# Hybrid diffusion step on one core: ScalarE copies the first pass of the second feed-forward product, and one first product takes high parts first

## What is computed

```python
def sq_relu_mlp(h, w1, w2):
    return jnp.square(jax.nn.relu(h @ w1)) @ w2
...
    for layer in range(DEPTH):
        ...
        hp = modulate(rmsnorm(xp, norm_ffn_pre[layer]), mod_p[3], mod_p[4])
        hs = modulate(rmsnorm(xs, norm_ffn_pre[layer]), mod_s[3], mod_s[4])
        xp = xp + mod_p[5] * rmsnorm(sq_relu_mlp(hp, w_ffn_in[layer], w_ffn_out[layer]), norm_ffn_post[layer])
        xs = xs + mod_s[5] * rmsnorm(sq_relu_mlp(hs, w_ffn_in[layer], w_ffn_out[layer]), norm_ffn_post[layer])
```

## Time and profile before

| what | value |
|---|---|
| median of 3 runs | 1427.66 us (1427.63 to 1428.13) |
| the profiled execution's own time | 1429.37 us |
| its span in the trace | 1427.3 us |
| TensorE matmuls busy | 1373.6 us, 96% |
| VectorE busy | 885.5 us, 62% |
| GpSimd busy | 715.1 us, 50% |
| ScalarE busy | 706.2 us, 49% |
| mean granted TensorE clock | 0.988 |

### The profile page before, as it was taken

The page is one execution under the profiler, slowest core; times in us unless marked ns, Lnnn a source line. Parts: engine busy times, 40 slices in busy tenths (PEclk is TensorE's granted clock), DMA queues, the critical chain, the costliest instruction groups (busy, mean ns, idle before and its releaser), DMA issues.

```text
span 1427.3 us, 20872 instructions
## 1 busy us (share of the span) xinstructions
PE 1373.6 (96%) x7682; PEld 1162.0 (81%) x7682; DVE 885.5 (62%) x1543; ACT 706.2 (49%) x1431; POOL 715.1 (50%) x547
## 2 busy tenths in 40 slices
PE   5999999989999999999999989999899999999998
PEld 3876787868888888989767867788789899899896
DVE  4477864866655565565663578627855655656646
ACT  4375824744434444443552367637544534444443
POOL 1430413775445556555352567635855565555550
PEclk8999999999999999999999999999999999999999
DMA  9534272533454412212455200034323222231213
GB/s 350 161 95 142 69 257 68 192 118 119 136 209 157 148 59 90 89 62 87 153 185 185 89 2 1 1 118 172 108 90 104 74 91 87 72 106 59 89 60 148
DMA packets 98059, 164.32 MB, mean 115 GB/s; under 512 B 11100, under 2 KB 49704, under 8 KB 97960
## 3 DMA queue, kind: packets, MB, share of 16 engines
q1 hardware_dynamic: 86320, 157.23, 32.4%
q10 hardware_dynamic: 11640, 5.76, 1.6%
HBM read 154.82 MB, written 8.16 MB: 114 GB/s over the span
## 4 chain that ended last, share of the span: by engine, by line
PE 45%; DVE 2%; POOL 2%; issue 1%; ACT 0%; DVEq 0%; POOLq 0%; ACTq 0%
PE PS L2025 13%; PE PS L2026 13%; PE PS L2027 13%; PE PS L2367 2%; PE PS L2356 1%; PE PS L2335 1%; PE PS L2075 1%; PE PS L2336 1%; PE PS L2319 0%; PE PS L2312 0%; POOL WLU L1592 0%; POOL GG L1538 0%; PE PS L2115 0%; POOL HL L1561 0%; DVE HF L1786 0%
## 5 line engine op out<-in xcount | busy, mean ns | idle before, releaser
L1592 POOL TENSOR_TENSOR WLU<-RAW,WHU 128x512 fp32r<-128x512 f32 x340 | 457.5, 1371 | 376.3 <-ACT WHU L1227 376.2
L1227 ACT CAST WHU<-RAW 128x512 fp32r<-128x512 f32 x340 | 197.3, 618 | 236.9 <-PE PS L2027 121.7
L2025 PE MATMUL PS<-WHU,MXR 128*128 128x512 f32 x640 | 254.6, 398 | 11.9 <-issue 9.8
L2026 PE MATMUL PS<-WLU,MXR 128*128 128x512 f32 x640 | 252.0, 394 | 0.0
L2027 PE MATMUL PS<-WHU,MXR 128*128 128x512 f32 x640 | 251.6, 393 | 0.0
L1934 DVE TENSOR_TENSOR ACC<-ACC,PS 128x512 f32<-128x512 f32 x260 | 177.6, 684 | 94.8 <-PE PS L2027 93.7
L1587 POOL TENSOR_TENSOR WL<-RAW,WH 128x512 fp32r<-128x512 f32 x84 | 117.5, 1432 | 212.9 <-ACT WH L1218 195.4
L2025 PE MATMUL PS<-HH,WHU 128*128 128x320 f32 (+2 forms) x576 | 178.8, 310 | 3.9 <-POOL HL L1561 3.9
L2027 PE MATMUL PS<-HH,WLU 128*128 128x320 f32 (+2 forms) x576 | 178.6, 310 | 0.0
L2026 PE MATMUL PS<-HL,WHU 128*128 128x320 f32 (+2 forms) x576 | 178.5, 310 | 0.0
L2025 PEld LDWEIGHTS PS<-WHU,MXR 128*128 128x128 f32 x640 | 121.1, 189 | 47.2 <-issue 17.9
(11 more groups left out here) (274 smaller groups left out, 2637.3 us busy)
## 6 DMA issues: line engine op xcount, KB each, us to landing
RAW<-in_w_ffn_in SPq DMA_DIRECT2D x32, 1024.0 KB, 5.5
RAW<-in_w_ffn_out SPq DMA_DIRECT2D x32, 1024.0 KB, 5.0
RAW<-in_w_mod SPq DMA_DIRECT2D x18, 1024.0 KB, 5.8
GG<-in_w_mod SPq DMA_DIRECT2D x13, 1024.0 KB, 7.4
MX<-in_w_mod SPq DMA_DIRECT2D x11, 1024.0 KB, 5.2
RAW<-in_w_in_even SPq DMA_DIRECT2D x7, 1024.0 KB, 5.3
RAW<-in_w_qkv SPq DMA_DIRECT2D x6, 1024.0 KB, 7.5
xd<-X SPq DMA_DIRECT2D x10, 512.0 KB, 8.0
```

What stands on the lines that cost most here:

```text
L1227: nc.scalar.copy(unit_view(WHU, u), unit_raw(u["ld"], u["of"])).then_inc(u_hi, 1)
L1592: nc.gpsimd.tensor_tensor(unit_view(WLU, u), unit_raw(u["ld"], u["of"]), unit_view(WHU, u).bitcast(f32), ALU.subtract)\
L2025: MM(out, wh, xh, start=first, stop=False, skip_group_check=reopens)
L2026: MM(out, wh, xl, start=False, stop=False, skip_group_check=reopens)
```

## The change

ScalarE takes over the ten copies of the first pass. The planner holds unit S3 of pair 2 back to event 16 (group 8 of the first pass; before, event 13 was the least). The direct product of p = 0, f = 0, part 1 waits for the high parts of its tokens alone, does its 16 matmuls on them, and then the 8 with the low parts of the tokens.

```diff
                     at = max(at, cycle + 9 if o[0] > 2 else NS + 5)
                 if o == (2, "S2"):
                     at = max(at, NS + 2)
+                if o == (2, "S3"):
+                    at = max(at, NS + 8)
...
+                elif k == "g" and not s["p"]:
+                    b = s["b"]
+                    act.wait_ge(t_add, 12 * s["layer"] + 12)
+                    upto(act, b_ready, b)
+                    nc.scalar.copy(ACC[:, s["t"], 512 * s["nh"]:512 * s["nh"] + 512], PS[:, 4 + b % 2, :]).then_inc(b_free[b % 2], 1)
...
-                elif k == "g":
+                elif k == "g" and s["p"]:
                     b, acc = s["b"], ACC[:, s["t"], 512 * s["nh"]:512 * s["nh"] + 512]
                     upto(dve, b_ready, b)
-                    if not s["p"]:
-                        dve.wait_ge(t_add, 12 * s["layer"] + 12)
-                    if s["p"]:
-                        V_.tensor_tensor(acc, acc, PS[:, 4 + b % 2, :], ALU.add).then_inc(b_free[b % 2], 1)
-                    else:
-                        V_.tensor_copy(acc, PS[:, 4 + b % 2, :]).then_inc(b_free[b % 2], 1)
+                    V_.tensor_tensor(acc, acc, PS[:, 4 + b % 2, :], ALU.add).then_inc(b_free[b % 2], 1)
...
-                    if p == 0 and f == 0:
+                    out = direct_bank(s)
+                    if (p, f, part) == (0, 0, 1):
+                        cols = DIRECT[1]
+                        for i in (0, 1):
+                            u = s["units"][i]
+                            pe.wait_ge(u_lo, u["number"] + 1)
+                            pe.wait_ge(f_hi[i], TT * layer + 5)
+                            for kt in range(4):
+                                for w in (WHU, WLU):
+                                    MM(out, unit_view(w, u)[:, kt, :], HH[:, 4 * i + kt, cols], start=w is WHU and (i, kt) == (0, 0), stop=False)
+                        for i in (0, 1):
+                            u = s["units"][i]
+                            pe.wait_ge(f_lo[i], TT * layer + 5)
+                            for kt in range(4):
+                                ins = MM(out, unit_view(WHU, u)[:, kt, :], HL[:, 4 * i + kt, cols], start=False, stop=(i, kt) == (1, 3))
+                        ins.then_inc(n_done, 1)
+                        continue
+                    if (p, f) == (0, 0):
                         for half in (0, 1):
-                            pe.wait_ge(f_lo[half], TT * layer + (2, 5)[part])
-                    out = direct_bank(s)
+                            pe.wait_ge(f_lo[half], TT * layer + 2)
```

## The result

The changed kernel takes 1431.97 us, the median of 20 runs; the kernel before took 1428.97 us in 20 runs beside them. The ratio is 1.0021 with a 95% interval of 1.0015 to 1.0027. So the change costs 3.0 us, where +1.2 was forecast. The prediction called 2.9 us the least that tells from no change; the measured difference lies 0.1 us above it, and its interval (2.1 to 3.9 us) on both sides of it.

What follows compares the result with a forecast made beforehand. TensorE, busy 96% of the span, was taken as the bound, with time to gain only in its waits and half clock. -11.4 + 4.2 + 6.8 + 1.6 = +1.2 us gave 1428.9 us, range 1420.5 to 1433.5.

Steps and rivals of the forecast that it cites:

- -11.4, the old waits: First pass: both 4-us waits for VectorE's copy and their half clock go; P1 6.2 and 5.2 us earlier.
- Group 2 waits 4.3 us behind comb1's cast: First pass: ScalarE's first copy stands behind that cast, so TensorE waits 4.3 us, swallowing the direct-product reordering's gain.
- +4.2, half clock behind it: First pass, behind the new group 2 wait: TensorE at 1.2 GHz costs 2.1 us a layer, bounds 0 and 2.6.
- +6.8, the second pass: Second pass: held-back S3 makes TensorE wait about 0.6 us at group 4 and 2.75 at group 5, 3.4 a layer.
- The chain of nine links: Second pass: late A11 cast of pair 3 delays GpSimd, S3 and group 3's addition; bank free at 24.6 us, wanted at 21.3.
- +1.6, half clock behind it: Second pass, behind its new waits: 1.2 GHz level costs 0.8 us a layer, bounds 0 and 2.6 in all.
- Part 1's reason: First pass: S3 of pair 2 is held back because its cast would hold up a copy on ScalarE.
- Costed at nothing: Pair 4's `w1` load, issued about 3 us later, and `w2` casts one event later: both put at no cost.
- The second pass without its wait: Rival: the chain to group 3 has slack, so no second-pass wait; -7.2 us, 1420.5; 0.27 including half the wait.
- The dearer clock: Rival: each of four new waits, at groups 2 and 5, is followed by 5.2 us half clock; +5.8, 1433.5 us; chance 0.22.
- The change did what it says: Rival denied this: first-pass TensorE waits for something other than VectorE's copy, old 4 us stay; +9, 1437 us; chance 0.03.

Runs made afterwards that it cites:

- e6: Changed kernel with the direct product back in its old order, waiting for the low parts again: 1429.19 us, 0.9998 of the kernel before.
- e2: Changed kernel, but VectorE copies groups 0 and 1 of the first pass: 1427.31 us, 0.9981 of the kernel before.
- e1: Changed kernel without holding back S3 of pair 2: 1423.02 us, 0.9954 of the kernel before.
- e7: Changed kernel without holding back S3 of pair 2, and with VectorE copying groups 0 and 1: 1425.72 us, 0.9976 of the kernel before.
- e12: Kernel before with only the copies moved to ScalarE: 1423.63 us, 0.9960 of the kernel before.
- e8: As e7, but VectorE copies four groups, pair 2's S2 and S1 come later, and pair 3 follows S3 after five events: 1423.53 us, ratio 0.9963.
- e11: VectorE copies four groups, S2 and S1 of pair 2 behind them, S3 behind P1, later units re-placed: 1426.76 us, 0.9979 of the kernel before.
- e5: Changed kernel with S3 of pair 2 held back one event instead of two: 1422.63 us, 0.9956 of the kernel before.
- e4: Kernel before with only the direct product's new order, high parts first: 1426.33 us, 0.9976 of the kernel before.

## Why the prediction was right, and where it was not

The measured +3.0 lies inside the stated range, but 0.1 us outside the band of -2.9 to +2.9 that had 0.48, and so in "slower", which had 0.25; the interval covers both.

**-11.4, the old waits.** Right to a tenth or two: e6 shows -6.3 and -5.3, with no half clock behind its waits at group 2. The reading that "issue" was VectorE's copy holds.

**Group 2 waits 4.3 us behind comb1's cast.** Measured 4.38 and 4.33, at the predicted time. e2 shows the cause by taking it away. Part 3's gain is swallowed, as said; e6 adds that it is less than nothing beside part 2.

**+4.2, half clock behind it.** To P1 the layers came out at -4.2 and -3.1, within 0.1 of the terms -6.2 + 2.1 and -5.2 + 2.1.

**+6.8, the second pass.** The chain of nine links held (A11's cast at 11.4 us, VectorE's idle time, the place of group 3's addition behind S3). The 0.6 us at group 4 did not come; group 5 has 3.26 instead of 2.75 in both layers, nearly their sum. Layer 0 has 0.72 us more at 345.50 (group 9), where VectorE's additions stand behind the turn's operations, which the prediction did not see. That is 7.2 us of new waits; two of 0.23 us that before has at group 6 are gone, so 6.8 are left, the forecast number.

**+1.6, half clock behind it.** This is the mis-sized term. It was the mean of one wait of 2.01 us with no drop and one of 1.88 with one. Both 3.26-us waits were followed by a drop, and of the second passes' +10.2 us 6.8 are waits, so about 3.4 us are left for it and for restarts. The forecast wait, 2.75 us, lay between the 2-us and the 4-us waits; only the shorter ones were priced in. This term makes the difference between +1.2 and the +2.8 of the stretches.

**Part 1's reason** was stated as clear: that S3's cast would hold up a copy. In the changed kernel it wouldn't (e1). It does where TensorE is earlier (e7, e12). **Costed at nothing**: the later load of pair 4's `w1` and the later `w2` units. Nothing of them shows behind the second passes of the changed kernel, where the difference stays within 0.1 us.

**The rivals.** The second pass without its wait is the kernel e1: -7.2 by the prediction, -6.6 measured by the ratio. The dearer clock came nearly halfway. The new waits' half clock cost about 2.1 us in each first pass (-4.2 and -3.1 beside e6's -6.3 and -5.3) and 3.4 in the second passes together, about 7.6 us in all; 5.8 were forecast, that rival had 10.4 and set its border at 7.5. The change did what it says: the 4-us waits of before are gone.

## What to carry to other kernels

Moving work to an engine that is idle "on average" helps only from the point at which that engine's program order lets it start; read what stands ahead of the first moved instruction, and leave the first ones where they were (two here; with four, e8 and e11, the next wait came). When a due time is changed in a planner, look at the first thing that follows it by a fixed distance, and ask in front of which block it used to stand: one event was 4.6 us here (e5), since the cast slid behind an activation that itself waits. And a gain that ends in front of a later wait is not neutral, if the wait becomes long enough for the clock to drop behind it.

## What the runs showed of the hardware

Over the feed-forwards of the 14 profiled executions (before, after, e1 to e12), TensorE's waits and the granted clock behind them sort like this. Of 11 waits of 1.26 to 1.74 us none was followed by 0.50. Of 14 waits of 1.88 to 2.95 us 7 were, and 7 were not, with no order by length: 1.88 was, 2.93 in e7's layer 0 was not, 2.95 in its layer 1 was. Of 25 waits of 3.26 to 4.46 us 24 were; the exception is 3.65 us in layer 1 of e4. So from 1.88 to 2.95 us half the waits were followed by a drop, and what decides it is not shown; from 3.26 us on nearly all were. That may be why executions of one kernel differ by some us (the changed one: 1430.06 to 1435.07), though only profiled ones show their waits. The same 3.26-us wait cost the second pass from 4.5 us (e6, layer 0) to 5.8 (e2, layer 0). The section of the Trainium skill named in the prediction (TensorE: Matmul & The Clock Gate, Why this matters for your kernels) lets gaps somewhat longer than 2 us pass; the seven waits of 1.88 to 2.95 us with a drop behind them disagree.

The subtraction L1651 took 0.67 us at 1056.23 in the changed kernel, where GpSimd starts only at 1057.01, and 1.67 us at 1061.07, while GpSimd was at work until 1062.18. The prediction's 1.18 lies between. What counts seems to be who starts first. Two more operations of the same shape in this trace, with GpSimd's:

```profile
1099.78 0.68 DVE L1644 TENSOR_TENSOR RAW<-RAW 128x512 f32<-128x512 f32 x1
...
1103.36 1.70 DVE L1649 TENSOR_TENSOR RAW<-RAW 128x512 f32<-128x512 f32 x1 [0.18 <-POOL WLU L1599]
```

```profile
1099.93 1.69 POOL L1599 TENSOR_TENSOR WLU<-RAW,WHU 128x512 fp32r<-128x512 f32 x1 [2.50 <-ACT WHU L1229]
1101.95 2.56 POOL L1599 TENSOR_TENSOR WLU<-RAW,WHU 128x512 fp32r<-128x512 f32 x2 [0.33 <-ACT WHU L1229]
```

VectorE starts 0.15 us ahead of GpSimd at 1099.78 and takes 0.68 us, and GpSimd's operation takes 1.69 instead of 1.28. At 1103.36 VectorE starts 0.15 us behind GpSimd's second operation (1103.21 to 1104.52) and takes 1.70. These are readings of one trace; no run changes the order of the two alone, so the cause is argued and not shown.
